# Value rows of an expert layer: a gather per row, or a dense weight matrix and a stream of the table

## The reference

```python
def one(hb):                                   # hb: h2 of some tokens (each has 1024 numbers)
    q = (hb @ w_query).reshape(..., 8, 2, 128) # 8 heads, two half keys
    s1 = einsum('thd,hkd->thk', q[:, :, 0], sub_keys[0])     # 128 scores per head and side
    s2 = einsum('thd,hkd->thk', q[:, :, 1], sub_keys[1])
    v1, i1 = top_k(s1, 16); v2, i2 = top_k(s2, 16)
    cand = v1[..., :, None] + v2[..., None, :]               # 256 sums
    best, sel = top_k(cand, 16)
    idx = i1[sel // 16] * 128 + i2[sel % 16]                 # one of 16384 experts
    gate = softmax(best)
    act = gelu(einsum('td,thkd->thk', hb, u_tab[idx]))
    return einsum('thk,thkd->td', gate * act, v_tab[idx])
x = x + gt2 * rms(one(h2), g_post2)
```

## Time and profile before

| | |
|---|---|
| median of 3 runs | 3824.27 us |
| profiled execution, span | 4199.6 us |
| time around the span in the profiled execution | not shown |
| before the first gather | 904.6 us |
| from the first gather to the end | 3295.0 us |
| busy: PE, DVE, POOL, ACT | 3314.8, 2313.6, 2152.0, 950.0 us |
| granted TensorE clock, mean | 0.881 |

### The profile page before, as it was taken

How to read it: one execution, slowest core, us unless ns; L and a number is a source line. 1 busy time by engine, 2 the same in 40 slices (tenths; PEclk the granted TensorE clock), 3 DMA queues, 4 the chain that set the end, 5 groups by cost and what they waited for, 6 DMA issues and landing times.

```text
span 4199.6 us, 38180 instructions
## 1 busy us (share of the span) xinstructions
PE 3314.8 (79%) x9348; PEld 1593.5 (38%) x9348; DVE 2313.6 (55%) x5821; ACT 950.0 (23%) x2161; POOL 2152.0 (51%) x2222
## 2 busy tenths in 40 slices
PE   8998989928777777877777777777777777887677
PEld 2454555513333333333333333333333333333222
DVE  2104552867755665555665655566555665556442
ACT  1003773312221221112112211211121121112111
POOL 0000300236566665666666666566666665666665
PEclk9999999969898898898888888888888888888888
DMA  9104102159999999999999999899999999999997
GB/s 357 64 15 126 32 19 113 61 188 352 344 357 359 353 359 354 347 368 343 341 359 347 350 356 344 332 354 355 360 347 358 358 357 348 343 363 358 361 362 303
DMA packets 365168, 1245.51 MB, mean 297 GB/s; under 512 B 52129, under 2 KB 57505, under 8 KB 362751
## 3 DMA queue, kind: packets, MB, share of 16 engines
q0 software_dynamic: 313504, 1141.02, 72.4%
q1 hardware_dynamic: 48852, 96.77, 6.6%
q10 hardware_dynamic: 2576, 5.10, 0.4%
HBM read 1220.34 MB, written 22.39 MB: 296 GB/s over the span
## 4 chain that ended last, share of the span: by engine, by line
PE 38%; issue 17%; another core or an unknown queue 9%; DVE 5%; DMA 4%; POOL 3%; ACT 1%; DVEq 0%; POOLq 0%; ACTq 0%; SPq 0%
PE ps_y L1692 33%; PE ps_q L950 5%; DMA urow<-in_u_tab,idx 3%; POOL urow L1473 2%; POOL vrow L1473 1%; DMA vrow<-in_v_tab,idx 1%; DVE urow L1612 1%; ACT diag L1580 1%; DVE aux L993 0%; PE ps_s L961 0%; DVE i L996 0%; DVE sel L996 0%; DVE i L992 0%; DVE aux L1029 0%
## 5 line engine op out<-in xcount | busy, mean ns | idle before, releaser
L1692 PE MATMUL ps_y<-vrow,diag 128*128 128x512 f32 (+1 forms) x4352 | 2220.8, 665 | 647.5 <-issue 329.9
L1612 DVE CUSTOM_DVE_ANT_0 urow<-urow,ps_h 128x1024 f32<-128x1024 f32 x1088 | 1299.8, 1220 | 1025.2 <-DMA urow<-in_u_tab,idx 865.6
L1692 PEld LDWEIGHTS ps_y<-vrow,diag 128*128 128x128 f32 (+1 forms) x4352 | 884.3, 209 | 1893.6 <-issue 1576.9
L1473 POOL DMA_INDIRECT vrow<-in_v_tab,idx x1088 | 1031.6, 948 | 785.7 <-issue 287.4
L1473 POOL DMA_INDIRECT urow<-in_u_tab,idx x1088 | 1030.7, 947 | 430.5 <-issue 282.8
L1580 ACT ACTIVATE diag<-const,wgt 128x128 f32<-128x128 f32 x1024 | 373.1, 396 | 1766.2 <-PE ps_y L1692 643.3
L950 PE MATMUL ps_q<-aux,w_q_sb 128*128 128x128 f32 x2048 | 271.7, 292 | 58.1 <-issue 49.4
L950 PEld LDWEIGHTS ps_q<-aux,w_q_sb 128*128 128x128 f32 x2048 | 263.9, 207 | 94.4 <-issue 93.2
L1293 POOL TENSOR_TENSOR xo<-xo,ot 128x1024 f32<-128x1024 f32 (+1 forms) x9 | 21.1, 2343 | 352.2 <-DVE ot L1249 352.2
L530 PE MATMUL ps_z<-hT,w_in_sb 128*128 128x512 f32 (+1 forms) x576 | 190.5, 491 | 4.6 <-DVE hT L448 4.6
L625 POOL MEMSET kTs<- 128x384 f32 x1 | 0.4, 418 | 322.7 <-POOLq L344 322.7
(11 more groups left out here) (181 smaller groups left out, 2341.3 us busy)
## 6 DMA issues: line engine op xcount, KB each, us to landing
ada<-in_w_ada SPq DMA_DIRECT2D x12, 2048.0 KB, 12.5
urow<-in_u_tab,idx POOLq DMA_INDIRECT x1088
vrow<-in_v_tab,idx POOLq DMA_INDIRECT x1088
w_in_sb<-in_w_in SPq DMA_DIRECT2D x8, 1024.0 KB, 17.9
w_q_sb<-in_w_query SPq DMA_DIRECT2D x8, 1024.0 KB, 14.3
x<-in_x_p ACTq DMA_DIRECT2D x8, 512.0 KB, 6.6
w_out_sb<-in_w_out SPq DMA_DIRECT2D x8, 512.0 KB, 7.0
xo<-in_x_p SPq DMA_DIRECT2D x8, 512.0 KB, 3.7
```

The lines of the kernel that those rows point to most:

```text
L1473: nc.gpsimd.indirect_dma_start(ring[k % RING][:, :], None, A[table][:, :], bass.IndirectOffsetOnAxis(ap=places[:, col:col + 1], axis=0)).t ...
L1612: nc.vector.tensor_tensor_reduce(out=urow[k % RING][:, :], in0=urow[k % RING][:, :], in1=ps_h[:, :], scale=1.0, scalar=0.0, op0=ALU.mult, ...
L1692: last = nc.tensor.matmul(ps_y[0:rows, c], diag[s % DIAGS][:, 0:rows], vrow[k % RING][:, c], start=(s == 0), stop=(s == PH * width(n) - 1))
```

## The change

The stage `experts` is new. In words:

* The order of the tiles changes: the prompt tiles come first and the sample tile last. `output` loses the sample's queries and searches.
* All queries and scores are computed at the start of `experts`, 512 tokens at a time, and the scores go to DRAM (`s_d`); ACT loads 128 KB of them back for each search. There are 24 steps of one head and 512 (or 64) tokens.
* `u_tab` rows are gathered as before, into a ring of 7, and DVE makes the same products. A *unit* is one tile and one head: 16 products, the search for the unit two later, the weights.
* `v_tab` rows of the prompt are gathered no more. For each pair of tiles (256 tokens; 4 pairs) a dense matrix of weights is built: 16384 experts x 256 tokens. The build takes 64 groups of 4 tokens. For each token, with its 128 slots on the partitions, `p1` is the one-hot of i2, `p2` the one-hot of i1 times the weight, and PE multiplies the two into a 128x128 block (`ps_dense`), which ACT copies to SBUF (`dense`) with two instructions per group. DVE makes `p1` of every group and `p2` of the even ones, POOL `p2` of the odd ones. The build of a pair is spread over the first 32 slots after the pair's last unit, two groups per slot.
* Then the whole of `v_tab` is streamed once for the pair, in 128 chunks of 128 rows (512 KB), by SP with a ring of 3. Per chunk PE does 4 matmuls of 512 columns. Their stationary operand is a slice `dense[...][:, t*P:(t+1)*P, c % 64]` of the matrix, whose columns lie 64 numbers (256 bytes) apart.
* The sample tile gathers its 64 `v_tab` buffers after its `u_tab` rows, and DVE adds them up with 64 multiply-adds.
* The loop is gone: every instruction is written out.

In the diff, the two functions `hot` are those of DVE and of POOL; the part with `ps_y` is PE's stream of one pair, and the last part is DVE's order.

```diff
-RING = 8
-DIAGS = 4
+URING = 7
+VRING = 3
+LA = 2
...
-            for t in range(NTILE - 1):
-                product(t)
...
-                for h in heads.get(t, []):
-                    find.search(own, dve, dve_passed, 0, h)
...
+            def hot(m, j):
+                for jj in (2 * j, 2 * j + 1):
+                    g = m * GROUPS + jj
+                    if jj == 0:
+                        dve.wait_ge(it_read, 2 * (m + 1))
+                    if g >= 2:
+                        dve.wait_ge(b_done, g - 1)
+                    last = nc.vector.tensor_tensor(p1[g % 2][:, :, :], iota[:, None, :].broadcast_to([P, 4, P]),
+                                                   iT[:, 1, 4 * jj:4 * jj + 4, None].broadcast_to([P, 4, P]),
+                                                   ALU.is_equal)
+                    if jj % 2 == 0:
+                        for t in range(4):
+                            col = 4 * jj + t
+                            last = nc.vector.tensor_scalar(p2[g % 2][:, t, :], iota, iT[:, 0, col:col + 1],
+                                                           wT[:, col:col + 1], ALU.is_equal, ALU.mult)
+                    last.then_inc(hot_dve, 1)
...
+            def hot(m, j):
+                g = m * GROUPS + 2 * j + 1
...
+                for t in range(4):
+                    col = 4 * (g - m * GROUPS) + t
+                    last = nc.gpsimd.tensor_scalar(p2[g % 2][:, t, :], iota, iT[:, 0, col:col + 1],
+                                                   wT[:, col:col + 1], ALU.is_equal, ALU.mult)
+                last.then_inc(hot_pool, 1)
...
+                pe.wait_ge(b_read, GROUPS * (m + 1))
+                if m:
+                    pe.wait_ge(y_done, 2 * m)
+                for c in range(NCH):
+                    j = m * NCH + c
+                    pe.wait_ge(v_full[j % VRING], chunk_full(j))
+                    for t in range(2):
+                        for half in range(2):
+                            last = nc.tensor.matmul(ps_y[t][:, 512 * half:512 * (half + 1)], dense[c // 64][:, t * P:(t + 1) * P, c % 64],
+                                                    vring[j % VRING][:, 512 * half:512 * (half + 1)],
+                                                    start=(c == 0), stop=(c == NCH - 1))
+                    last.then_inc(v_used, 1)
...
+            for u in range(UNITS):
+                products(u)
+                if u + LA < UNITS:
+                    search(u + LA)
+                weights(u)
+            sample_rows()
+            tail()
+            finish(NT - 2)
+            finish(NT - 1)
```

More of the change, by code:

```diff
@@ L1468, in _ @@
+            for m in range(PAIRS):
+                for c in range(NCH):
+                    if c == VRING and m > 0:
+                        finish(m - 1)
+                    chunk(m * NCH + c)
+            finish(PAIRS - 1)
+            sp.wait_ge(y_out, 16 * NT)
         @block.gpsimd
         def _(pool):
-            def gather(table, ring, full, n, h, k):
-                col = width(n) * h + k
-                places = idx0 if is_sample(n) else idx
-                nc.gpsimd.indirect_dma_start(
-                    ring[k % RING][:, :], None, A[table][:, :],
-                    bass.IndirectOffsetOnAxis(ap=places[:, col:col + 1], axis=0)).then_inc(full[k % RING], 16)
@@ new lines, in _ @@
+            for u in range(UNITS):
+                pool.wait_ge(idx_ready, u + 1 if not is_sample(u) else NT * PH + 2 * (u - NT * PH + 1))
+                for k in range(width(u)):
+                    places = idx0[:, slots(u) - NQ + k:slots(u) - NQ + k + 1] if is_sample(u) else idx[u % 4][:, k:k + 1]
+                    gather("u_tab", slots(u) + k, places)
+                    if build_step(u, k):
+                        hot(*build_step(u, k))
+            for k in range(SLOTS // 2):
+                gather("v_tab", NSLOT + k, idx0[:, k:k + 1])
@@ new lines, in unit, with h2T_out @@
+            def unit(u):
+                do_gelu(u)
+                if u % PH == PH - 1 and u + 1 < UNITS:
+                    copy_h2((u + 1) // PH)
+                if u + LA < UNITS:
+                    exp_gate(u + LA)
+            def h2T_out(t):
+                n = tile_rows(t)
+                for half in range(2):
+                    act.wait_ge(tr_done, 2 * t + half + 1)
+                    nc.scalar.activation(h2T[:, 4 * half:4 * half + 4, t * P:t * P + n],
+                                         ps_y[0][:, 512 * half:512 * (half + 1)]
+                                         .rearrange("p (k t) -> p k t", k=4)[:, :, 0:n], ACT.Copy).then_inc(tr_read, 1)
@@ new lines, in _ @@
+            h2_load(0)
+            for t in range(4):
+                h2T_out(t)
+            copy_h2(0)
+            nu = 0
+            for i, (g, h) in enumerate(hsteps):
+                queries_out(i)
+                if i:
+                    scores_out(i - 1)
+                if g < 2 and h >= 4:
+                    for t in qgroups[g + 1][2][h - 4:h - 3]:
+                        h2T_out(t)
+                if 1 <= i <= 3:
+                    s_load(i - 1)
+                    if i >= 2:
+                        exp_gate(i - 2)
+                if i >= 4 and i % 2 == 0:
+                    s_load(nu + 3)
+                    unit(nu)
+                    nu += 1
```

958 lines of the change are left out of this document (503 added, 455 removed).

## The result

The changed kernel takes 4396.24 us (median of 4 runs, 4392.39 to 4406.15) where the kernel before takes 3822.57 beside it. The ratio is 1.1503, with an interval of 1.1487 to 1.152: 15% slower. That is 621 us over the forecast and outside its range.

What follows compares the result with a forecast made beforehand. The prediction took the gathers (DMA) to bound the part from the first gather. Start, first pair, three build-and-stream regions, last build and end: 870 + 477 + 3 x (187 + 445) + 208 + 322 = 3773, forecast 3775 us, range 3600 to 3980.

Steps and rivals of the forecast that it cites:

- First pair: First 16 units, without a stream: paced by DVE at 29.8 us a unit, gathers hidden, 477 us.
- The build slot: Each of a build's 32 slots takes 4.7 us, between 3.5 and 6.0; a build region is 187 us.
- four instructions at an eighth of 2926 ns plus start, 0.4 each: POOL's one-hot work in a build slot, which with a gather of 0.94 + 0.30 makes 2.9 us.
- The chunk on PE is 4 x 0.43 = 1.72 us: PE's need per streamed chunk at the high clock, 3.44 us at the low one; also used for the end.
- The stretches: Streams beside 14 units: 36.6 us a streamed unit, 404 us a stream, 493 us a region; 445 in run terms.
- the division by 1.128: Everything paced by DMA is 1.128 times faster in the runs than in the profiled execution; a region 445 us, not 493.
- Until the first product: Output stage at 11.6 us per tile, `experts` beginning near 805, then 65 us: first product at 870.
- Rival (a): Builds and searches exclude each other with POOL: build slot 6.0 us instead of 4.7, +166, so 3940 us; chance 0.26.
- Rival (b): DVE is never starved: streamed units near 29.8 us, end 128 x 1.72 + 20, total 3610 us; chance 0.22.
- Rival (c): The stationary operand's strided load bounds the stream: 3.7 us a chunk, total 4034 us; chance 0.08.
- Rival (d): The value traffic of gathers and chunks isn't really cut: total near 3824 us; chance 0.02.
- the two signs named as proof of a wrong forecast: A unit without stream taking over 33 us, or a stream outlasting its 14 units.

Runs made afterwards that it cites:

- pool_ahead: The changed kernel with POOL making the one-hots of a build slot 4 gathers later; 4184.21 us.
- p2_dve: The changed kernel with DVE making all one-hots and POOL only gathering; 4030.53 us.
- half_cols: The changed kernel with each matmul of the stream taking 256 of its 512 columns, chunks still loaded whole; 4319.45 us.
- half_both: The changed kernel with each stream chunk loading 512 of its 1024 columns and each matmul taking 256 of them; 4127.01 us.
- before_again: The kernel before, unchanged, profiled once more; 3824.3 us.
- adjacent: The changed kernel with the stream's stationary operand read as 128 adjacent numbers instead of 256 bytes apart; 4390.52 us.
- p2_split_timed: The changed kernel with POOL making two of eight `p2` per slot, two buffers, four gathers late, DVE six; 3972.74 us, ratio 1.0397 to the kernel before.

## Why the prediction was wrong, step by step

* **First pair: right.** 477.4 against 477, unit 28.6 to 31.1 us after the first one; the DVE work worked out from the earlier trace rows was right.
* **The build slot: failed,** in the step "four instructions at an eighth of 2926 ns plus start, 0.4 each". The row taken has one width and not the other: such an instruction of 128 columns takes 0.79 us in the middle case and 0.89 in the mean. The second fault is in the form of the estimate. The work was summed engine by engine, while the added waits tie the engines into a circle; the gather behind POOL's one-hots was counted for its issue (0.94 + 0.30) and not for who waits for it. pool_ahead puts the gather's place at 1.7 us a slot, p2_dve puts POOL's whole part at 2.9. Cost: 268 us over the four builds. A third term was short as well, "PE's 8 small matmuls at 0.12 us": they are 16 passes, and PE was busy with them 3.7 us a slot (473.5 us over 128 slots), mostly at the low clock, and its part of each group stands in the circle.
* **"The chunk on PE is 4 x 0.43 = 1.72 us": failed.** It is 8 x 0.43 = 3.44. In the page of the kernel before, the row of `L1692` has x4352 for 1088 slots of two matmuls, so the records showed it:

```profile
L1692 PE MATMUL ps_y<-vrow,diag 128*128 128x512 f32 (+1 forms) x4352 | 2220.8, 665 | 647.5 <-issue 329.9
```

  Cost: the end, which was 154 us too long. half_cols lets it shrink by 96 us; half_both, with the traffic halved as well, by 152. So the rest of the 154 is the traffic's share, again forecast too fast.
* **The stretches: the split was right and its conversion wrong.** The forecast had, in the traced terms, 36.6 us for a streamed unit, 404 for the stream and 493 for the region. half_cols, whose PE takes the assumed 1.72 us a chunk, has about 36.5, 416 to 426 and, in the table's terms, some 495 (506 from one-hot to one-hot, less the 10 to 12 by which the two measures differ). With PE's real need the chunks come a little slower (3.68 us) and the gathers get more: 34.5 us a unit, 480 to 490 a region. The step that failed is the division by 1.128: it was also laid on the 393 GB/s of the earlier trace rows, which is already what the chip gives (397 in before_again, 393 in the new stream). 3 x (493 - 445) = 144 us too little, of which 119 came.
* **Until the first product: failed, since PE was left out of the sum.** The forecast took the chain through ACT and POOL for the output stage. With the search gone the stage is bound by PE, whose 512-column matmuls are two passes each here too. Its timeline in the changed kernel:

```profile
742.42 3.60 PE L1115 MATMUL ps_a<-w_out_sb,oT 128*128 128x512 f32 x8
745.86 3.60 PE L1115 MATMUL ps_b<-w_out_sb,oT 128*128 128x512 f32 x8
749.29 1.84 PE L1105 MATMUL ps_n<-ones,sq 128*128 128x1 f32 x16
...
757.94 3.60 PE L1115 MATMUL ps_a<-w_out_sb,oT 128*128 128x512 f32 x8
```

  PE works without a gap, and from one tile to the next (742.42 to 757.94) are 15.5 us, not 11.6. In them lie 32 passes of 512 columns, 13.8 us; at one pass per matmul it would be 6.9. The experts begin at 838 instead of 805, and the first product comes 109 us later instead of 65, with PE busy 87 of them. This part was read from the trace and not tested by a run.
* **Rival (a)** had the right place and a wrong mechanism. DVE's `p1` takes 0.69 us beside POOL as without it, a search during a stream still takes 9.6 us (1745.95 to 1755.55), and the slot of 7.7 us is above even the 6.0 of this rival. What stood in the way was mainly a wait. The two engines do disturb each other, but in the changed kernel it is POOL that is stretched: the 246 `p2` of POOL with no DVE instruction beside them take 0.79 us, and so do those beside a product; the 54 that lie mostly beside a `p1` take 1.31 in the mean, and 63 beside DVE's `p2` 1.11. That is 0.1 us in the mean of 512, some 0.4 a slot.
* **Rival (b)** had a chance of 0.22. Where it looked, at whether rows would come late with two queues, the answer is 34.5 us a unit: they do. Its end, 128 x 1.72 + 20, had the chunk at half of PE's real need.
* **Rival (c)** is refuted by adjacent. The row shows 296 ns for the load with a step of 256 bytes and 191 without. The Trainium skill (SBUF — State Buffer, Door 1: The DMA port swizzle, the note on "cachelines") says that each access to a new 16-byte line pays a penalty. By that rule the load is dearer, and the trace agrees: 1.55-fold. It doesn't reach the time, because the load lies beside a pass.
* **Rival (d)** is refuted: the changed kernel moves 999.53 MB, the kernel before 1245.51.
* Neither of the two signs named as proof of a wrong forecast came: a unit without stream takes 29.5 us, and the streams end 13 to 19 us before the next build needs PE, though 90 were forecast. Both looked at the parts that were understood. The signs that told were the slot (7.7 us with one search in it, against "4.7"), the first product (947 us against 870) and the count of records.

What even the best version lacks can be worked out. From the first gather the kernel before keeps DMA full for 2916 us at 397 GB/s, 1158 MB. p2_split_timed, from its first product to its end:

```profile
947.20:3958.20 3011.00, 2422.55 (x7032) 1656.87 (x7032) 2398.46 (x6139) 465.15 (x956) 1391.07 (x1401) 0.90 0.80 299
```

These are 900 MB, which would need 2268 us at 397 GB/s, 648 less than before. It takes 3011, so 743 us are lost: DMA is at less than half in the first build (0.45, with builds of 135, 145, 144 and 165 us), at seven tenths in the last stream and at eight in the first pair. More is lost in these than was saved.

## What to carry to other kernels

Count an operation's records against its instructions before multiplying by a duration: here each float32 matmul was two, and that doubled what a stream costs PE. When a change puts work and a wait in front of an instruction that feeds another engine, follow the circle of waits from that instruction back to itself; its length, not the fullest engine's sum, is the period. And a saving in traffic is worth only what lies where the traffic bounds: check that the new stages keep the queue full, and look separately at the last one, which has nothing beside it.

## What the runs showed of the hardware

* A `TENSOR_SCALAR` of 128x128 float32 with two per-partition operands took 0.79 us on POOL in the middle case and 0.34 on DVE; one in twenty took about 1.37 us or more on POOL and 0.42 on DVE. Its time on POOL went with what DVE did beside it: 0.79 us beside nothing or a product, 1.31 mostly beside a `TENSOR_TENSOR` of 128x512. In p2_split_timed, where DVE was always busy, the mean was 1.15, and one in twenty of DVE's `p1` took 0.93 us or more where 0.69 is usual.
* A float32 matmul showed two records, 0.43 us each at 512 columns and 0.22 at 256, at a granted clock of 1.00. At 128 columns they were 0.112 apart at the upper level of the clock and 0.213 at the lower.
* A weight load of 128 columns took 191 ns with adjacent columns and 296 ns at a step of 256 bytes.
* Over a whole stage, gathers alone moved 397 GB/s, and gathers and a stream together 393 to 400.
* The granted clock was 0.56 to 0.58 in builds where PE was busy half the time in short pieces, 0.72 in p2_dve and 0.84 in p2_split_timed, both with PE busy some 0.65 of the time.

What stays open: how much of the later start is the output stage's PE and how much the query steps, since no run changed either; how much of a build is the low clock, since no run changed it alone; and what disturbed the first profiled execution.
